# Two models in one kernel: convolution sums in PSUM, modulation products inside the input phase, tanh gates in the attention rounds, and other seams between the sublayers

## The chip, the cores and the metric

The kernel runs on one core of one Trainium2 chip, in one launch. The metric is the device time of that core in microseconds (us).

## The reference

Two models run one after the other on 256 tokens of 1024 numbers, all float32. The first has two layers. In each, one large product gives everything that its four branches need:

```python
h = x @ w_in[l]
(rw_p, rw_g, q_lat, kv_lat, k_pe, mla_g, conv_u, conv_g, xq, xg, merge) = jnp.split(h, SPLIT_POINTS, axis=-1)
y_rwkv = _rwkv7_branch(...)          # recurrent state over 256 steps
y_mla = _mla_branch(...)             # rms norm of two latents, then q, k, v, causal attention
y_conv = _conformer_conv_branch(...) # GLU, causal depthwise convolution of width 31, LayerNorm, swish
y_mem = _memory_xattn_branch(...)    # attention into 256 memory tokens
proj = jnp.einsum('bsnc,ncd->bsnd', branches, w_o_branch[l])
gates = jax.nn.sigmoid(merge.reshape(B, S, N_BRANCH, D) + b_gate[l])
merged = jnp.sum(gates * proj, axis=2)
x = _layer_norm(DEEPNORM_ALPHA * x + merged @ w_out[l], ln_g[l], ln_b[l])
```

The second model has two layers of three sublayers (a gated feed-forward, an attention mix, a gated feed-forward) over the tokens and a context of 256 rows. Each sublayer starts with an rms norm, is shifted and scaled by rows of a modulation product `silu(c) @ w_mod + b_mod` (nine rows for the tokens and nine for the context), and ends with `h + weight * gate * rms_norm(y)`.

## The kernel before

**First model.** All weights come in panels of 128 partitions by 2048 float32 (1 MB), 96 for each layer, in an order fixed ahead by `stream_of_a_layer`. The SP queue loads them into a ring of four slots (`m_ring`): a panel is fetched when the panel four places earlier has been used by PE (the semaphore `panel_used`). The products of two panels land in PSUM banks 0 and 1, taken in turn (`TURNS`, `USE`). PE waits on `bank_free0` or `bank_free1` until ACT or DVE has emptied the bank. Six other banks, A(0) to A(5), serve the attention, the norms and the recurrent branch.

A layer has these stages. The *input phase* takes 24 panels ("in"). ACT copies each to a rounded type (`high`, L755, to `m_ws`, three buffers), POOL subtracts that copy from the panel (L294), PE multiplies the two halves (`split_panel`, L377 to L379, 48 matmuls), and ACT moves the sum to `hT` (L780). Then comes a stretch in which the convolution's sum is finished by DVE (31 taps, L1007, four instructions for each tap in SBUF, begun during the input phase), and its norm and the norms of the latents run by turns on PE, ACT and DVE. After it come the products for q, k and v (`lat` panels), four attention rounds (two into the tokens, two into the memory), the preparation of the recurrent branch, its two halves, and a tail with the last gates.

The second model's modulation rows are worked out in the first model's layers: `mod_rows(w)` uses four "mod" panels with 32 columns of weights (PE L326, both banks, then ACT copies each bank to `mrow`), and `mod_columns(w)` turns two rows into columns (PE L337, ACT L735). Nine pairs of rows are taken in each layer: the first two in the stretch after the input phase, the others in the rounds and in the preparation. `gate(q, p)` (L346, a panel each) and `branch(q)` (L356, one panel) are the merge's products. DVE multiplies them (`merge`, L987) in the order of `MERGE_ORDER`.

**Second model.** 160 panels come through a ring of two. POOL rounds each (L1570) and subtracts (L1572). A sublayer starts with `norm_in`: DVE scales the tokens (L1997), PE makes rows (L1625) and transposes (L1633), ACT copies each of eight chunks, DVE rounds and subtracts each (L2001, L2003, semaphore `aT_split`). Then `hidden` runs the panels (L1616 to L1618, 48 matmuls for each). At the end, `norm_out` squares on ACT (L1864), takes the root (L1868) and lets DVE apply it (L2015) and add it to the tokens or to the context (L2019).

Of the kernel before, what the change touches and what calls it, by code (L numbers as in the profile page):

```python
# [32 lines left out]
MERGE_ORDER = (2, 3, 4, 5, 6, 7, 0, 1)  # L33


PANEL, USE, TURNS = {}, {}, [0, 0]
# [15 lines left out]
def stream_of_a_layer():  # L52

    def pair(w):
# [4 lines left out]
    feeds(*[("mem", n) for n in range(4)])  # L59
    feeds(*[("in", n) for n in range(24)])  # L60
    for n in list(range(4)):
        turn(n % 2, ("mem", n))
    for n in range(24):
        turn(n % 2, ("in", n))
    for w in range(PAIRS):
        if w == 2:
            feeds(*[("lat", n) for n in range(4)])
        pair(w)
        turn(w % 2, ("col", w))
    for q in MERGE_ORDER:  # L70
        feeds(("gate", q, 0), ("gate", q, 1), ("branch", q))
        for p in range(2):
            turn(p, ("gate", q, p))
        for b in range(2):
            turn(b, ("branch", q, b))
    feeds(*[("out", n) for n in range(4)])
# [82 lines left out]
def first_model(nc, io, x_tok, mod, out=None):  # L159

    with ExitStack() as ctx:  # L161
# [17 lines left out]
        small = sb("small", [P, 192])  # L179
        with ExitStack() as place:  # L180
            work = place.enter_context(nc.sbuf_tensor("m1_work", [P, 73 * T], F32))
# [22 lines left out]
        eps6, eps5, eps_gn = small[:, 180:181], small[:, 181:182], small[:, 182:183]  # L204
        ln_rows = hT[:, 20:28, :].rearrange("p u t -> p (u t)")
        mrow = brT[:, 0:KW, :].rearrange("p k t -> p (k t)")
# [5 lines left out]
        lat_sq, lat_n = units(44, 5), units(49, 5)  # L212
# [31 lines left out]
        def sgate(t):  # L244
# [4 lines left out]
            "slot0 slot1 slot2 slot3 loaded c_in c_act mcol_ps vec_in rows_in x_in out_st panel_used bank_free0 bank_free1 "  # L249
# [49 lines left out]
        def _(pe):  # L299
# [5 lines left out]
            with pe.Fori(0, DEPTH) as l:  # L305
# [106 lines left out]
                pe.wait_ge(s["c_act"], 1)  # L412
                mod_rows(0)
                pe.wait_ge(s["conv_acc"], l + 1)
                for k in range(KW):
                    last = mm(A(0)[:, 0:T], c("ones"), conv[:, k, :], start=(k == 0), stop=(k == KW - 1))
                last.then_inc(s["mean_ps"], 1)
                pe.wait_ge(s["csq_in"], l + 1)
                for k in range(KW):
                    last = mm(A(1)[:, 0:T], c("ones"), conv_sq[:, k, :], start=(k == 0), stop=(k == KW - 1))  # L420
                last.then_inc(s["var_ps"], 1)


                pe.wait_ge(s["lat_sq_in"], l + 1)
                pe.wait_ge(s["xT_sb"], 8 * l + 8)
                for j, (u0, n) in enumerate(((0, 3), (3, 2))):
                    for k in range(n):
                        last = mm(A(2)[:, j * T:(j + 1) * T], c("ones"), lat_sq[:, u0 + k, :],
                                  start=(k == 0), stop=(k == n - 1))
                last.then_inc(s["lat_ps"], 1)  # L430
                mod_columns(0)
                mod_rows(1)
                pe.wait_ge(s["lat_n_in"], l + 1)
# [5 lines left out]
                for h in range(HEADS):  # L439
                    out = A(1 + h // 2)[:, (h % 2) * T:(h % 2 + 1) * T]  # L440
# [6 lines left out]
                for h in range(HEADS):  # L447
# [6 lines left out]
                    if h % 4 == 3:  # L454
                        last.then_inc(s["k_ps"], 1)
                w = panel(("lat", 2))
# [12 lines left out]
                for a in range(4):  # L469
# [13 lines left out]
                    mod_columns((1, 3, 5, 6)[a])  # L483
                    mod_rows((2, 4, 6, 7)[a])
# [6 lines left out]
                    if a < 2:  # L491
                        mod_columns(2 + 2 * a)
                        mod_rows(3 + 2 * a)
# [13 lines left out]

                mod_columns(7)
                mod_rows(8)
# [9 lines left out]
                mod_columns(8)  # L519
                gate(2, 0)  # L520
                pe.wait_ge(s["o_done"], 4 * l + 4)
                pe.wait_ge(s["ksq_in"], l + 1)
# [4 lines left out]
                gate(2, 1)  # L527
                branch(2)
                gate(3, 0)
                gate(3, 1)  # L530
# [34 lines left out]
                for i in range(NT):  # L565
# [5 lines left out]
                    for g in range(4):  # L571
# [10 lines left out]
                        if g == 1:  # L582
                            gate(4 + i, i)
                        elif g == 3 and i == 0:
                            gate(4, 1)
                        elif g == 3:
                            branch(5)
# [43 lines left out]
                    if i == 0:  # L631
                        pe.wait_ge(s["conv_done"], l + 1)
                        branch(4)
                    else:
                        gate(6, 0)
# [26 lines left out]
                    gate(5 + i, i)  # L662
# [17 lines left out]
                branch(6)  # L680
                gate(7, 0)
# [6 lines left out]
                gate(7, 1)  # L688
                branch(7)
                gate(0, 0)  # L690
                gate(0, 1)
                pe.wait_ge(s["rw_done"], l + 1)
                branch(0)
                gate(1, 0)
                gate(1, 1)
# [15 lines left out]
        def _(act):  # L711
# [8 lines left out]
            with act.Fori(0, DEPTH) as l:  # L720
# [16 lines left out]
                def gate(q, p):  # L737
# [5 lines left out]
                    for u in range(2):  # L743
                        last = a_(sgate(t)[:, 2 * p + u, :], bank[:, p, u * T:(u + 1) * T], ACT.Sigmoid,
                                  bias=v("b_gate", q * 4 + p * 2 + u))
# [30 lines left out]
                for n in range(24):  # L776
                    if n + 2 < 24:
                        high(n + 2)
# [1449 lines left out]
```

## Time and profile before

| what | value |
|---|---|
| median of 3 runs | 3427.41 us (3423.55 to 3431.52) |
| the profiled execution | 3424.13 us, span 3421.9 us |
| PE busy | 2970.3 us, 87% |
| DVE, ACT, POOL busy | 1259.0, 706.6, 1256.1 us |
| mean granted clock of PE | 0.93 |
| layer 1: input phase | 42.3 to 179.0 us |
| layer 1: stretch between input phase and q | 179.0 to 240.1 us, PE busy 21.4 us |
| layer 1: q, k, v | 240.1 to 264.4 us |
| layer 1: four rounds | 264.4 to 347.5 us |
| layer 1: preparation | 347.5 to 426.6 us |
| layer 1: two halves | 426.6 to 585.9 us |
| layer 1: tail up to the output panels | 585.9 to 662.0 us |

The profile is of one execution, and its stages add up to its span. Layer 2 has the same stages at close to the same lengths (its stretch between input and q is 60.3 us). A stage is as long as the chain that runs through it, and PE's idle time in it says how far PE is from being that chain.

### The profile page before, as it was taken

To read this page: it belongs to the slowest core of one execution; us is meant where nothing else is said; L and a number is where in the kernel's file an instruction comes from. 1 tells how busy PE (TensorE), PEld (TensorE's weight loads), DVE (VectorE), ACT (ScalarE), POOL (GpSimd) and SP (SyncE) were. 2 spreads that over 40 slices of the span, in tenths; PEclk is the share of its full clock that TensorE was granted. 3 is DMA by queue.
4 is the path that set the end of the run, shared out by engine and by line. 5 is a ranking of instruction groups with operands and counts; after the bars stand their busy time and mean duration, and the time that the engine had idled before them with its cause. 6 is when DMAs were issued, how large, how long until landed. Compare 5 with 4: busy or idle time off the path is not lost.

```text
span 3421.9 us, 41743 instructions
## 1 busy us (share of the span) xinstructions
PE 2970.3 (87%) x16084; PEld 2443.6 (71%) x16084; DVE 1259.0 (37%) x1702; ACT 706.6 (21%) x1327; POOL 1256.1 (37%) x531
## 2 busy tenths in 40 slices
PE   8957799999577999599997988899979999697797
PEld 7934688789346886388775766688757878586695
DVE  2962734149628331400134163200341012515327
ACT  3413111033231110210112142211121111204211
POOL 4800000057000000266563503366544665371595
PEclk9978899999788999799998977999989999899899
DMA  6537411445383113322221202122221222130343
GB/s 220 186 140 291 152 62 62 147 168 186 133 304 149 51 62 123 112 98 97 82 92 53 94 1 68 49 98 98 86 74 67 94 97 86 62 111 25 111 172 123
DMA packets 67453, 383.80 MB, mean 112 GB/s; under 512 B 19072, under 2 KB 20736, under 8 KB 21888
## 3 DMA queue, kind: packets, MB, share of 16 engines
q1 hardware_dynamic: 66464, 379.19, 31.4%
q10 hardware_dynamic: 864, 2.84, 0.2%
q8 instruction: 91, 1.49, 0.2%
q14 instruction: 34, 0.28, 0.0%
HBM read 380.96 MB, written 1.05 MB: 112 GB/s over the span
## 4 chain that ended last, share of the span: by engine, by line
issue 32%; POOL 9%; POOLq 8%; PE 5%; DMA 2%; SPq 1%; DVE 1%; ACT 1%; DVEq 0%; ACTq 0%
POOL m_ws L1572 8%; POOLq L1571 7%; PE m_bank L1661 2%; DMA m_ring<-in_panels 2%; SPq L1525 1%; POOL m_ws L1590 1%; POOLq L1584 1%; POOLq L1589 1%; PE m_bank L1804 0%; PE m_bank L1616 0%; PE m_bank L1617 0%; PE m_bank L1618 0%; PE m_bank L1782 0%; PE m_bank L1769 0%; PE m_bank L1734 0%
## 5 line engine op out<-in xcount | busy, mean ns | idle before, releaser
L1616 PE MATMUL m_bank<-m_aT,m_ws 128*128 128x512 f32 (+1 forms) x1664 | 607.0, 365 | 52.3 <-DVE m_aT_low L2003 37.5
L1617 PE MATMUL m_bank<-m_aT_low,m_ws 128*128 128x512 f32 (+1 forms) x1664 | 603.8, 363 | 0.0
L1618 PE MATMUL m_bank<-m_aT,m_ws 128*128 128x512 f32 (+1 forms) x1664 | 603.2, 363 | 0.0
L1572 POOL TENSOR_TENSOR m_ws<-m_ring,m_ws 128x2048 fp32r<-128x2048 f32 x127 | 594.5, 4681 | 18.7
L1661 PE MATMUL m_bank<-m_ws,m_hs 128*128 128x512 f32 x1848 | 437.8, 399 | 38.5 <-DVE m_hs L2049 28.3
L294 POOL TENSOR_TENSOR m_ws<-m_ring,m_ws 128x2048 fp32r<-128x2048 f32 x48 | 225.0, 4692 | 624.3 <-ACT m_ws L755 624.2
L1661 PEld LDWEIGHTS m_bank<-m_ws,m_hs 128*128 128x128 f32 x1848 | 355.7, 193 | 120.4 <-issue 39.4
L1616 PEld LDWEIGHTS m_bank<-m_aT,m_ws 128*128 128x128 f32 x1664 | 317.3, 191 | 104.7 <-issue 34.2
L1583 POOL TENSOR_TENSOR m_small<-m_small 128x1 f32<-128x1 f32 x158 | 30.6, 194 | 923.1 <-PE m_bank L1618 503.2
L1618 PEld LDWEIGHTS m_bank<-m_aT,m_ws 128*128 128x128 f32 x1664 | 317.3, 191 | 48.1
L1617 PEld LDWEIGHTS m_bank<-m_aT_low,m_ws 128*128 128x128 f32 x1664 | 317.6, 191 | 47.6
L2040 DVE TENSOR_TENSOR m_hidT<-m_sg,m_bank 128x512 f32 (+1 forms) x88 | 54.6, 621 | 770.5 <-ACT m_sg L1879 770.5
L346 PE MATMUL m_bank<-m_xF,m_ring 128*128 128x256 f32 x1024 | 235.3, 391 | 43.0 <-DVE m_hT L987 40.4
L1570 POOL TENSOR_SCALAR m_ws<-m_ring 128x2048 fp32r<-128x2048 f32 x127 | 244.2, 1923 | 28.7 <-issue 19.9
L346 PEld LDWEIGHTS m_bank<-m_xF,m_ring 128*128 128x128 f32 x1024 | 198.9, 196 | 74.1 <-DVE m_hT L987 43.6
L1007 DVE SCALAR_TENSOR_TENSOR m_work<-m_work,m_vec 128x256 f32<-128x256 f32 x240 | 226.8, 1005 | 31.9 <-issue 31.9
L377 PE MATMUL m_bank<-m_xT,m_ws 128*128 128x256 f32 x768 | 216.0, 281 | 1.4 <-ACT m_work L773 1.4
L379 PE MATMUL m_bank<-m_xT,m_ws 128*128 128x256 f32 x768 | 217.1, 283 | 0.0
L2049 DVE TENSOR_TENSOR m_hs<-m_hidT,m_hs 128x512 fp32r<-128x512 f32 (+1 forms) x80 | 133.3, 1671 | 226.5 <-ACT m_hs L1888 226.4
L378 PE MATMUL m_bank<-m_xT_low,m_ws 128*128 128x256 f32 x768 | 213.5, 278 | 0.0
L1566 POOL MEMSET m_small<- 128x1 f32 x1 | 0.1, 98 | 538.9 <-POOLq L161 538.9
L377 PEld LDWEIGHTS m_bank<-m_xT,m_ws 128*128 128x128 f32 x768 | 144.3, 188 | 3.0 <-ACT m_work L773 3.0
(348 smaller groups left out, 3971.1 us busy)
## 6 DMA issues: line engine op xcount, KB each, us to landing
m_ring<-in_panels SPq DMA_DIRECT2D x352, 1024.0 KB, 4.8
m_bias<-in_rpb SPq DMA_DIRECT2D x48, 64.0 KB, 2.4
m_hT<-in_ln_rows ACTq DMA_DIRECT2D x2, 1024.0 KB, 6.4
m_con<-in_con SPq DMA_DIRECT2D x1, 1408.0 KB, 13.8
m_memT<-in_memT SPq DMA_DIRECT2D x1, 1024.0 KB, 5.9
x_tok<-in_x SPq DMA_DIRECT2D x1, 1024.0 KB, 14.4
m_ctx_tok<-in_ctx SPq DMA_DIRECT2D x1, 1024.0 KB, 4.8
out<-x_tok SPq DMA_DIRECT2D x1, 1024.0 KB, 4.0
```

Of the source, the lines that this page charges most:

```text
L294: nc.gpsimd.tensor_tensor(ws[:, c_ % 3, 1, :], ring[:, PANEL[("in", c_)] % RING, :], ws[:, c_ % 3, 0, :].bitcast(F32), ALU.subtract).then_ ...
L346: last = mm(out[:, u * T:(u + 1) * T], w[:, u, k, :], xF[:, k, :], start=(k == 0), stop=(k == KD - 1))
L377: mm(dst, w[:, 0, u, k, :], xT[:, k, :], start=(k == 0), stop=False)
L379: last = mm(dst, w[:, 1, u, k, :], xT[:, k, :], start=False, stop=(k == KD - 1))
L1007: V.scalar_tensor_tensor(conv[:, k, :], padded[:, k, bass.ds(tap, T)], vec[:, bass.ds(tap * KW + (VEC1["conv_w"] + k), 1)], conv[:, k, :], ...
L1570: nc.gpsimd.tensor_scalar(ws[:, p, 0, :], ring[:, p, :], 1.0, 0.0, ALU.mult, ALU.add)
L1571: pool.drain()
L1572: nc.gpsimd.tensor_tensor(ws[:, p, 1, :], ring[:, p, :], ws[:, p, 0, :].bitcast(F32), ALU.subtract)\
L1616: mm(out, w, a, start=start, stop=False)
L1617: mm(out, w, a_low, start=False, stop=False)
L1618: return mm(out, w_low, a, start=False, stop=stop)
L1661: last = mm(bank[:, 2 * i + hf, :], lhs[:, at], rhs[:, hf * 512:(hf + 1) * 512], start=start and q == 0, stop=stop and q == 2)
```

## The change

1. The order of the panels and of the banks' turns is new. Rows 0 to 3 of the modulation are taken inside the input phase, after input panels 3, 7, 11 and 15, and columns 0 to 3 after panels 5, 9, 13 and 18. Rows 4 come between the products for k and v, rows 5 to 8 in rounds 2 and 3 and in the preparation. Gates and branches 4 and 5 are taken in rounds 0 and 1, and `MERGE_ORDER` follows.
2. The sums of the latents' squares are taken on PE after input panel 8, the convolution's mean after 19 and its variance after 21. Their roots on ACT and the rest on DVE follow inside the input phase. Some buffers move to a new tile `ext`, so that nothing is shared that is still in use.
3. The convolution's running sum lies in A(0) and A(1), in PSUM. The last tap writes to SBUF.
4. A gate is the tanh of half its argument, and the merge multiplies (gate + 1) by the product. The residual's factor is doubled and the epsilon of the layer norm is four times as large, so that the result is the same.
5. Second model: the first panel of each sublayer runs k outside and u inside (`first_unit_panel`), and waits for the first two of the eight chunks rather than for all. `norm_out` keeps the product in its PSUM bank and adds it from there, and starts with a square root of a constant.
6. The scratch area for generated descriptors is set to 1024.

```diff
+MERGE_ORDER = (4, 5, 2, 3, 6, 7, 0, 1)
+ROWS_AFTER, COLUMNS_AFTER = (3, 7, 11, 15), (5, 9, 13, 18)
...
+    for n in range(24):
+        feeds(("in", n))
+        turn(n % 2, ("in", n))
+        if n in ROWS_AFTER:
+            rows(ROWS_AFTER.index(n))
+        if n in COLUMNS_AFTER:
+            columns_of(COLUMNS_AFTER.index(n))
...
                 for n in range(24):
                     split_panel(n, free(("in", n))).then_inc(s["panel_used"], 1)
-
+                    if n in ROWS_AFTER:
+                        pe.wait_ge(s["c_act"], 1)
+                        mod_rows(ROWS_AFTER.index(n))
+                    if n in COLUMNS_AFTER:
+                        mod_columns(COLUMNS_AFTER.index(n))
...
+                mod_rows(7)
+                gate(2, 0)
                 mod_columns(7)
-                mod_rows(8)
+                gate(2, 1)
 
                 pe.wait_ge(s["tanh_in"], l + 1)
...
                 pe.wait_ge(s["o_done"], 4 * l + 4)
+                branch(2)
                 pe.wait_ge(s["ksq_in"], l + 1)
...
                 for n in range(24):
-                    if n + 2 < 24:
+                    if n + 2 < 24 and n + 1 not in ROWS_AFTER:
                         high(n + 2)
+                    if n - 1 in ROWS_AFTER:
+                        mod_rows(ROWS_AFTER.index(n - 1))
+                    if n - 1 in COLUMNS_AFTER:
+                        mod_columns(COLUMNS_AFTER.index(n - 1))
                     used(("in", n))
                     a_(hT[:, 2 * n:2 * n + 2, :], bank[:, n % 2, :].rearrange("p (u t) -> p u t", t=T),
                        ACT.Copy if n < 16 else ACT.Silu).then_inc(bank_free[n % 2], 1)
+                    if n + 1 in ROWS_AFTER:
+                        high(n + 2)
...
                         V.scalar_tensor_tensor(tap_sum(k), padded[:, k, bass.ds(tap, T)],
                                                vec[:, bass.ds(tap * KW + (VEC1["conv_w"] + k), 1)], tap_sum(k),
                                                ALU.mult, ALU.add)
...
+            def first_unit_panel(e, b, tokens):
+
+                w = ws[:, b, :, :].rearrange("p h (u k c) -> p h u k c", u=2, k=KD)
+                for k in range(KD):
+                    pe.wait_ge(s["aT_split"], KD * e + max(k, 1) + 1)
+                    for u in range(2):
+                        last = parts(bank[:, u, 0:tokens[u]], w[:, 0, u, k, :], w[:, 1, u, k, :],
+                                     aT[:, k, 0:tokens[u]], aT_low[:, k, 0:tokens[u]], k == 0, k == KD - 1)
+                return last
...
             def norm_out(e, tiles, last_panel):
+                a_(small[:, 62:63], eps, ACT.Sqrt)
...
-                        V.tensor_tensor(tok(i), tok(i), y[:, i, :], ALU.add).then_inc(s["x_new"], 1)
+                        V.tensor_tensor(halves(tok(i)), halves(tok(i)), bank[:, 2 * i:2 * i + 2, :], ALU.add)\
+                            .then_inc(s["x_new"], 1)
```

The first place is ACT's queue around input panel 3, of the kernel before. `m_ws<-m_ring` is the rounding of a coming input panel, `m_hT<-m_bank` the emptying of a bank, and "slot" waits are for a load.

```order
L755 ACTIVATE m_ws<-m_ring 128x2048 [waits m1_slot0]
L722 REGISTER_ALU
L780 ACTIVATE m_hT<-m_bank 128x512 [waits m1_panel_used]
L755 ACTIVATE m_ws<-m_ring 128x2048 [waits m1_slot1]
L722 REGISTER_ALU
L780 ACTIVATE m_hT<-m_bank 128x512 [waits m1_panel_used]
L784 ACT_TABLE_LOAD
L784 ACTIVATE m_hT<-m_hT 128x1024
L755 ACTIVATE m_ws<-m_ring 128x2048 [waits m1_slot2]
L722 REGISTER_ALU
L780 ACTIVATE m_hT<-m_bank 128x512 [waits m1_panel_used]
```

In the changed kernel two roundings (of input panels 4 and 5) stand ahead of the emptying of panel 3's bank, and a third (of panel 6) ahead of the copies of the modulation rows (`m_ext<-m_bank`).

```order
L800 ACTIVATE m_ws<-m_ring 128x2048 [waits m1_slot0]
L800 ACTIVATE m_ws<-m_ring 128x2048 [waits m1_slot1]
L766 REGISTER_ALU
L829 ACTIVATE m_hT<-m_bank 128x512 [waits m1_panel_used]
L835 ACT_TABLE_LOAD
L835 ACTIVATE m_hT<-m_hT 128x1024
L800 ACTIVATE m_ws<-m_ring 128x2048 [waits m1_slot2]
L766 REGISTER_ALU
L773 ACTIVATE m_ext<-m_bank 128x512 [waits m1_panel_used]
L766 REGISTER_ALU
L773 ACTIVATE m_ext<-m_bank 128x512 [waits m1_panel_used]
```

The second place is PE's queue behind the 48 matmuls of input panel 3, in the changed kernel. Before, the wait on `split_in` and the matmuls of panel 4 stood there directly.

```order
L349 REGISTER_ALU [waits m1_c_act]
L355 REGISTER_ALU [waits m1_slot0]
L366 MATMUL m_bank<-m_ring,m_cact 32x512 [waits m1_bank_free0]
L366 MATMUL m_bank<-m_ring,m_cact 32x512 x3
L366 MATMUL m_bank<-m_ring,m_cact 32x512 [waits m1_slot1]
L366 MATMUL m_bank<-m_ring,m_cact 32x512 x3
L355 REGISTER_ALU [waits m1_slot2]
L366 MATMUL m_bank<-m_ring,m_cact 32x512 [waits m1_bank_free1]
L366 MATMUL m_bank<-m_ring,m_cact 32x512 x3
L366 MATMUL m_bank<-m_ring,m_cact 32x512 [waits m1_slot3]
L366 MATMUL m_bank<-m_ring,m_cact 32x512 x3
L355 REGISTER_ALU
```

Now sixteen products of the modulation and their waits stand ahead of panel 4: two for loads whose slots come free late, and one for each bank.

The third place is the start of a sublayer's first panel on PE. Before, one wait for all chunks stands ahead of it:

```order
L1648 UNCONDITIONAL_BRANCH [waits m2_aT_split]
L1648 ISA
L1616 MATMUL m_bank<-m_aT,m_ws 128x512 [waits m2_h_free,m2_split_in]
L1617 MATMUL m_bank<-m_aT_low,m_ws 128x512
L1618 MATMUL m_bank<-m_aT,m_ws 128x512
```

In the changed kernel it waits for each chunk, and the first wait is for two:

```order
L1681 MATMUL m_bank<-m_aT,m_ws 128x512 [waits m2_aT_split,m2_h_free,m2_split_in]
L1682 MATMUL m_bank<-m_aT_low,m_ws 128x512
L1683 MATMUL m_bank<-m_aT,m_ws 128x512
L1681 MATMUL m_bank<-m_aT,m_ws 128x512
L1682 MATMUL m_bank<-m_aT_low,m_ws 128x512
L1683 MATMUL m_bank<-m_aT,m_ws 128x512
L1681 MATMUL m_bank<-m_aT,m_ws 128x512 [waits m2_aT_split]
L1682 MATMUL m_bank<-m_aT_low,m_ws 128x512
L1683 MATMUL m_bank<-m_aT,m_ws 128x512
L1681 MATMUL m_bank<-m_aT,m_ws 128x512
```

The waits moved from the head of the panel to the six matmuls of each chunk.

## Rows read from the trace of the kernel before

**Rows 1.** PE timeline, 179 to 240 us: start, duration, operation, idle before, releaser.

```profile
180.73 2.78 PE L326 MATMUL m_bank<-m_ring,m_cact 128*32 128x512 f32 x24
...
211.72 3.78 PE L416 MATMUL m_bank<-m_work,m_con 128*128 128x256 f32 x8 [26.63 <-DVEq L1011]
...
224.55 1.84 PE L337 MATMUL m_bank<-m_con,m_brT 128*128 128x2 f32 x16
...
240.11 12.32 PE L442 MATMUL m_bank<-m_work,m_ring 128*128 128x256 f32 x48 [9.71 <-DVE m_work L1033]
```

**Rows 2.** Ring loads issued at 179.2, 183.7 and 185.3 us: time to landing.

```profile
DMA to landing us min/median/max: 4.8/4.8/4.8
...
DMA to landing us min/median/max: 8.1/8.1/8.1
...
DMA to landing us min/median/max: 9.0/9.0/9.0
```

**Rows 3.** ACT timeline in the input phase, 145 to 152 us.

```profile
145.46 1.91 ACT L755 ACTIVATE m_ws<-m_ring 128x2048 fp32r<-128x2048 f32 x1
150.65 0.60 ACT L780 ACTIVATE m_hT<-m_bank 128x512 f32<-128x512 f32 x1 [3.28 <-PE m_bank L379]
```

**Rows 4.** DVE timeline, convolution taps with POOL busy, then idle.

```profile
159.74 9.77 DVE L1007 SCALAR_TENSOR_TENSOR m_work<-m_work,m_vec 128x256 f32<-128x256 f32 x4 [0.54 <-issue]
...
172.25 1.67 DVE L1007 SCALAR_TENSOR_TENSOR m_work<-m_work,m_vec 128x256 f32<-128x256 f32 x4 [0.53 <-issue]
```

**Rows 5.** Page, part 5: the convolution taps of both layers.

```profile
L1007 DVE SCALAR_TENSOR_TENSOR m_work<-m_work,m_vec 128x256 f32<-128x256 f32 x240 | 226.8, 1005 | 31.9 <-issue 31.9
```

**Rows 6.** PE timeline, RWKV preparation of layer 1.

```profile
354.90 2.96 PE L516 MATMUL m_bank<-m_work,m_lora 64*128 64x256 f32 x16
...
370.72 1.89 PE L524 MATMUL m_bank<-m_work,m_con 128*128 128x256 f32 x8
...
404.27 15.63 PE L346 MATMUL m_bank<-m_xF,m_ring 128*128 128x256 f32 x64 [17.84 <-DVE m_hT L987]
...
426.64 1.91 PE L303 MATMUL m_bank<-m_con,m_work 128*128 128x128 f32 x16
```

**Rows 7.** DVE timeline: the key norm's wait in the preparation.

```profile
374.19 0.69 DVE L1109 TENSOR_SCALAR m_work<-m_work 128x1024 f32<-128x1024 f32 x1 [6.41 <-ACT m_work L860]
```

**Rows 8.** PE timeline, the end of layer 1's gates.

```profile
616.49 14.08 PE L346 MATMUL m_bank<-m_xF,m_ring 128*128 128x256 f32 x64 [0.78 <-DVE m_hT L987]
630.40 7.07 PE L356 MATMUL m_bank<-m_brT,m_ring 128*128 128x256 f32 x32
```

**Rows 9.** PE timeline, one sublayer seam of the second model.

```profile
1820.16 5.57 PE L1625 MATMUL m_bank<-m_prob,m_con 128*128 128x512 f32 x8 [17.25 <-DVE m_prob L1987]
...
1837.74 0.80 PE L1616 MATMUL m_bank<-m_aT,m_ws 128*128 128x512 f32 x1 [7.88 <-DVE m_aT_low L2003]
```

**Rows 10.** DVE timeline of that seam.

```profile
1804.12 7.63 DVE L2019 TENSOR_TENSOR x_tok<-x_tok,m_y 128x1024 f32<-128x1024 f32 x2
...
1815.48 2.36 DVE L2019 TENSOR_TENSOR m_ctx_tok<-m_ctx_tok,m_y 128x1024 f32<-128x1024 f32 x2
...
1830.38 0.69 DVE L2003 TENSOR_TENSOR m_aT_low<-m_hidT,m_aT 128x512 fp32r<-128x512 f32 x1
```

**Rows 11.** POOL timeline of that seam.

```profile
1805.39 5.28 POOL L1572 TENSOR_TENSOR m_ws<-m_ring,m_ws 128x2048 fp32r<-128x2048 f32 x1
1850.53 0.19 POOL L1583 TENSOR_TENSOR m_small<-m_small 128x1 f32<-128x1 f32 x1 [39.86 <-PE m_bank L1618]
```

**Rows 12.** Windows of that seam: span, PE busy, granted clock, DMA share.

```profile
1824.00:1834.00 10.00, 5.45 (x36) 1.00 0.01 2
1834.00:1842.00 8.00, 4.26 (x12) 0.57 0.00 0
```

**Rows 13.** ACT timeline: the table load ahead of the norm's square root.

```profile
1798.68 1.28 ACT L1868 ACT_TABLE_LOAD   x1
```

**Rows 14.** Page, part 5: PE idle before the first panels of the sublayers.

```profile
L1616 PE MATMUL m_bank<-m_aT,m_ws 128*128 128x512 f32 (+1 forms) x1664 | 607.0, 365 | 52.3 <-DVE m_aT_low L2003 37.5
```

More of the change, by code:

```diff
@@ L52, in stream_of_a_layer, with rows @@
 def stream_of_a_layer():
-    def pair(w):
+    def rows(w):
         feeds(*[("mod", 4 * w + n) for n in range(4)])
@@ L57, in pair, with columns_of, gates @@
             turn(b, ("row", 2 * w + b))
[L59 to L68, printed above, removed]
+    def columns_of(w):
         turn(w % 2, ("col", w))
-    for q in MERGE_ORDER:
+    def gates(q):
         feeds(("gate", q, 0), ("gate", q, 1), ("branch", q))
@@ L75, in stream_of_a_layer @@
             turn(b, ("branch", q, b))
+    feeds(*[("mem", n) for n in range(4)])
+    for n in range(4):
+        turn(n % 2, ("mem", n))
+    for n in range(24):
[5 more added lines that the diff above has]
+            columns_of(COLUMNS_AFTER.index(n))
+    feeds(("lat", 0), ("lat", 1))
+    rows(4)
+    feeds(("lat", 2), ("lat", 3))
+    columns_of(4)
+    gates(4)
+    gates(5)
+    for w in (5, 6):
+        rows(w)
+        columns_of(w)
+    rows(7)
+    turn(0, ("gate", 2, 0))
+    columns_of(7)
+    turn(1, ("gate", 2, 1))
+    for b in range(2):
+        turn(b, ("branch", 2, b))
+    feeds(("gate", 2, 0), ("gate", 2, 1), ("branch", 2))
+    rows(8)
+    turn(0, ("gate", 3, 0))
+    columns_of(8)
+    turn(1, ("gate", 3, 1))
+    for b in range(2):
+        turn(b, ("branch", 3, b))
+    feeds(("gate", 3, 0), ("gate", 3, 1), ("branch", 3))
+    gates(6)
+    for q in (7, 0):
+        for p in range(2):
+            feeds(("gate", q, p))
+            turn(p, ("gate", q, p))
+    feeds(("branch", 7), ("gate", 1, 0), ("gate", 1, 1), ("branch", 0), ("branch", 1))
+    for name in (("branch", 7), ("gate", 1), ("branch", 0), ("branch", 1)):
+        for b in range(2):
+            turn(b, name + (b,))
     feeds(*[("out", n) for n in range(4)])
@@ L421, in _ @@
[L421 to L432, printed above, removed]
@@ L1104, in _ @@
                 V.memset(AR[64:128, :, :, 2, :], 0.0)
+                merge(2)
+                dve.wait_ge(s["wa_in"], l + 1)
+                for k in range(KW):
+                    V.tensor_scalar(k2[:, k, :], sa[:, k, :], 1.0, v("k_a", k), ALU.subtract, ALU.mult)
                 dve.drain()
@@ L1723, in _ @@
                         pe.wait_ge(s["f_free"], 8 * l + n - 1)
-                    unit_panel((n0 + n) % 2, 2 * (n % 2), [T2 if full or 2 * n + u >= F_AK else T for u in range(2)])\
-                        .then_inc(s["used"], 1)
+                    tokens = [T2 if full or 2 * n + u >= F_AK else T for u in range(2)]
+                    if n == 0:
+                        last = first_unit_panel(e, n0 % 2, tokens)
+                    else:
+                        last = unit_panel((n0 + n) % 2, 2 * (n % 2), tokens)
+                    last.then_inc(s["used"], 1)
                 for n in range(2):
```

259 lines of the change are left out of this document (144 added, 115 removed).

## The prediction

> **What bounds the kernel now.** I read the page first, then PE's timeline by stages, then the waits where PE stands. PE is busy 87% of the span, so most of the time is PE's own work, and only the stretches where it stands can give anything. Layer 1 has four kinds. The stretch of 61.1 us behind the input phase (60.3 in layer 2) holds 21.4 us of PE work: PE waits 26.63 us for the end of the convolution on DVE, then for the norm [rows 1]. The rounds and the preparation of the recurrent branch are chains on DVE and ACT, with one hole of 17.84 us [rows 6]. In the tail PE runs gates and branches back to back [rows 8]. In the second model each seam between sublayers leaves PE standing 17.25 us for the norm of the last product and 7.88 us for the eight chunks [rows 9].
>
> **First model, input phase.** This is where the change can lose. The order shows four modulation panels between input panels 3 and 4, and the ring holds four panels. I count from the moment PE ends input panel 3, t = 0. The 16 products cost 2.78 / 24 x 32 = 3.7 us of PE [rows 1]. A lone load lands after 4.8 us; issued behind others it takes 8.1 and 9.0 us, and as these two were issued 1.6 us apart, each lands 2.5 us behind the one before it [rows 2]. At t = 0.15 the slot of panel 3 is refilled with the fourth "mod" panel, landing at 5.0. The first two are used by 1.0 and 1.9, so input panel 4 is issued at 1.15 and lands at 7.5, and panel 5, issued at 2.05, at 10.0. ACT's queue has the rounding of 4 (7.55 to 9.45) and of 5 (10.05 to 11.95), 1.91 us each, ahead of the emptying of panel 3's bank, 0.60 us [rows 3]. So bank 1 is free at 12.6, and the third and fourth "mod" products run from 12.6 to 14.5. Only then are the slots for input panels 6 and 7 free: panel 6 is issued at 13.75 and lands at 18.6. Its rounding, to 20.5, stands ahead of the copy of the modulation row, which frees bank 0 at 21.1. PE starts input panel 4 at 21.2. POOL's part of panel 4, with the 5.28 us of such an instruction [rows 11], is over by 15 and does not decide. With the columns, 1.84 us and their wait, 2.2 in all [rows 1], an insertion costs 23.4 us, of which some 6 are work. Four make 93.6.
>
> The latents' sums, mean and variance cost 2.2, 1.9 and 1.9 us of PE in the phase (10 matmuls of the L416 kind, and 4 each: the row has eight in 3.78 us, at the lower clock [rows 1]). After such a gap I expect the clock to come back late: the gates behind the 17.84 us hole took 15.63 us against 14.08 for the same 64 matmuls [rows 6, 8], so 1.6 for each gap, 6.4. The phase grows by 93.6 + 6.0 + 6.4 + 0.7 of small hand-overs = 106.7 us, the stretch of 61.1 goes, and 1.9 of transposes stay: **q starts 47.5 us later**.
>
> The convolution's place in PSUM earns nothing here. Even at the mean of 1005 ns [rows 5], the 120 instructions of a layer take 113 us of DVE beside the input phase that now lasts 243, and the mean is asked for only after panel 19. That cover is thick: without it, the taps under POOL at 9.77 us for four against 1.67 [rows 4] would stand in the way as before.
> The Trainium skill (SBUF — State Buffer, the section on its two separate sides) says that a VectorE instruction with two SBUF inputs and a GpSimd one lock each other out for the whole instruction; the tap in PSUM has one SBUF input and so escapes, which the two rows for four taps fit.
>
> **First model, the rest.** Between k and v the four products of rows 4 cost 3.7, and the two last "lat" panels are issued only as they free slots: they land 8.5 and 11.0 after the products' start by the spacing above, which costs waits of 4.8 and 0.9: +9.4. In the rounds gates and branches take the place of modulation products under the waits for the softmax; two gates, 14.1, are a little longer than the cover, and I take +1.4 between -5 and +5. In the preparation, L516 stood 7.4 us behind the rounds' end (354.90 - 347.5). Now rows 7 (3.7), gate(2,0) (7.07), a column pair (1.84) and gate(2,1) (7.07) stand ahead, 19.7 us, and about 3.9 for the landing of gate(2,0)'s panel: 23.6. Behind it come L516 (2.96), branch(2) (7.07), L524 (1.89) and ACT's 1.1 to the start of DVE's chain at 374.19: 36.6. From there to 426.64 it was 52.45 [rows 6, 7], less merge(2), 1.3, now ahead: 87.8, with 0.2 of hand-over 88.0 against 79.1: +8.9. The clock after the hole: +1.6. In the second half branch(5), 7.07 [rows 8], goes from a place where DVE's masks cover a part: between 0 and 7.07, I take half, -3.6. The tail loses four gate panels and one branch, five times 7.07: -35.3. Sum for a layer: 47.5 + 9.4 + 1.4 + 8.9 + 1.6 - 3.6 - 35.3 = +29.9, **two layers +60** (bounds +35 and +80: stalls of 18 and 24 us for 21.2, the preparation from 0 to +12). The tanh gates change no count that PE or ACT waits for.
>
> **Second model.** At a seam the first panel started at 1837.74 and ended at 1850.5, 12.8 us, because the clock was at 0.57 from 1834 to 1842 [rows 9, 11, 12], after PE had stood 7.88 us. Now it starts when the second chunk is split, at 1830.38 + 0.69 = 1831.1 [rows 10], while the clock is 1.00 (1824 to 1834), and DVE delivers a chunk each 1.1 us against 1.35 that PE takes for one (10.8 for the panel at full clock), so PE never waits again. It ends at 1842.3: 8.2 earlier. Five sublayers show this wait, 37.5 us together [rows 14]; four are like this one (32.8), the first gives about 6, the sixth waits for another thing: -38.8. In `norm_out` the addition to the tokens took 7.63 us under POOL's 5.28 and that to the context 2.36 without it [rows 10, 11]. With the product in PSUM it should take the short time, but the small two-input operations of the next pair of tiles then stand where POOL's instruction still runs, until 1810.7: I take 1.8 of the 5.3, four times, -7.2. The dummy root pulls the table load, 1.28 [rows 13], off the last norm: -1.3, and -0.2 for small things. **Second model -47.5** (bounds -35 and -54).
> By the rule of the Trainium skill named above, the addition is free of the lock and the next small one is not; the sum would be the same -7.2.
>
> Sum: 3424.1 + 59.8 - 47.5 = 3436.4 for an execution like the profiled one. The runs' median lies 3.3 above it, so **3440 us**.
>
> **The rivals.**
> (A) As worked out, 3433 to 3450. For it: ACT's order is fixed, and each step is a row. 0.5.
> (B) The refill is shorter. If two loads issued 0.9 us apart don't queue, panel 5 lands at 6.9 and each insertion costs 18.1 + 2.2, 8 x 3.1 = 25 less: 3415. If the clock also stays up, 8 x 1.6 = 13 less: 3402. Against it: the 8.1 and 9.0 us [rows 2]. This one ends faster. It decides from a stall of 20.4 us for each insertion downward if no other term moves by more than 10. 0.15.
> (C) The seam gives all of the 5.3 us four times, 14 more: 3426, the same as before. For it: the context's 2.36; against it: POOL's instruction still runs. 0.13.
> (D) The change does not stall: if the rounding of panels 4 and 5 came early, an insertion would cost its work, about 9 us, and 8 x 14.4 = 115 less gives 3325. It would need a ring that holds more than the order shows. 0.05.
> (E) More is lost: landings of 9.0 us in the rounds too (gate and branch panels are taken at 7.07 each, three in a row), 8 more for each layer, or table loads of 1.28 by turns between silu, root and tanh inside the phase, about four for each layer: 3455 to 3465. 0.17.
>
> **How the numbers follow.** This kernel's measurement tells 0.2%, 6.9 us. Faster (below 3420.5): B and D, and some of C: 0.22. Same: C and the low edge of A: 0.18. Slower: the rest of A, and E: 0.60. The range from 3404 to 3464 takes in A, C, most of B and of E.
>
> **What the new profile should show.** Between input panels 3 and 4 PE has two gaps, the first of about 10 us before the third "mod" product, the second of about 7 us, ended by ACT's copy of a row. Input phases of about 243 us. No idle stretch for the convolution. The tail 35 us shorter. The first panels of sublayers start about 6.6 us earlier, at full clock. I am wrong if the gap is not near 21 us, if DVE's convolution ends after panel 19, or if the seams give less than 6 us each.

## The result and the profile after

The changed kernel takes 3473.45 us (median of 4 runs, 3467.78 to 3474.25), against 3426.64 us before (4 runs): a ratio of 1.0132, with an interval of 1.0114 to 1.0149. It is 46.8 us slower, outside the range that I gave. The head of the page after:

```profile
span 3465.8 us, 41711 instructions
...
PE 2986.7 (86%) x16084; PEld 2461.0 (71%) x16084; DVE 1118.9 (32%) x1705; ACT 710.5 (20%) x1335; POOL 1248.8 (36%) x531
```

PE has 44 us more span and 16 us more busy time. By stages of layer 1, read from PE's timelines of both kernels (the last column is from the prediction):

| stage, layer 1 | before | after | difference | predicted |
|---|---|---|---|---|
| first input panel to q | 197.9 | 256.1 | +58.2 | +47.5 |
| q, k, v | 24.3 | 35.9 | +11.7 | +9.4 |
| four rounds | 83.1 | 83.3 | +0.2 | +1.4 |
| preparation | 79.2 | 91.4 | +12.2 | +10.5 |
| halves and tail | 235.4 | 199.4 | -36.0 | -38.9 |
| output panels, and the start | | | -3.1 | 0 |
| sum | | | +43.2 | +29.9 |

Up to the second model's first row products the whole first model is 89.3 us longer (1487.74 against 1398.45 us), so layer 2 loses 46.1. From there to the end it is 1978.1 against 2023.4 us: -45.4, predicted -47.5.

**The insertion.** PE's timeline of the changed kernel between input panels 3 and 4 (start, duration, operation, idle before and its releaser):

```profile
63.67 1.92 PE L366 MATMUL m_bank<-m_ring,m_cact 128*32 128x512 f32 x16
77.24 3.59 PE L366 MATMUL m_bank<-m_ring,m_cact 128*32 128x512 f32 x16 [11.65 <-ACT m_hT L829]
86.71 0.58 PE L417 MATMUL m_bank<-m_xT,m_ws 128*128 128x256 f32 x1 [5.88 <-ACT m_ext L773]
```

Two "mod" products, a hole of 11.65 us, two more, a hole of 5.88 us, and then panel 4: 23.0 us after panel 3's end at 63.74. The order of events was predicted with 10.7 and 6.7 us. ACT's timeline of the same place tells who held PE:

```profile
72.32 1.91 ACT L800 ACTIVATE m_ws<-m_ring 128x2048 fp32r<-128x2048 f32 x1 [13.59 <-DMA m_ring<-in_panels]
74.79 1.91 ACT L800 ACTIVATE m_ws<-m_ring 128x2048 fp32r<-128x2048 f32 x1 [0.57 <-DMA m_ring<-in_panels]
76.61 0.58 ACT L829 ACTIVATE m_hT<-m_bank 128x512 f32<-128x512 f32 x1
...
84.19 1.91 ACT L800 ACTIVATE m_ws<-m_ring 128x2048 fp32r<-128x2048 f32 x1 [4.58 <-DMA m_ring<-in_panels]
86.00 1.07 ACT L773 ACTIVATE m_ext<-m_bank 128x512 f32<-128x512 f32 x2
```

L800 rounds panels 4 and 5. It waited 13.59 us for the load of the first, and 0.57 for that of the second. Only then comes L829, which empties bank 1, though PE's sum had been lying there since 63.74. L800 of panel 6 stands ahead of the two copies of the modulation rows (L773) in the same way. Panel 4 landed 8.6 us after panel 3's end (I had 7.5), panel 5 11.05 (I had 10.0). The waits of the whole kernel, by who ends them (sum, times, longest):

```profile
PE m_bank L1690 <- DVE m_prob L2075: 98.9, 6, 26.1
PE m_bank L366 <- ACT m_hT L829: 88.1, 8, 11.8
PE m_bank L417 <- ACT m_ext L773: 47.8, 8, 6.4
```

There are 88.1 + 47.8 = 135.9 us in sixteen holes of a kind that was not there before. The windows show the clock (span, PE busy, granted clock, DMA share, GB/s; 1.00 is 2.4 GHz, 0.50 is 1.2 GHz, and a value between them is the mean of a window that holds both):

```profile
40.00:64.00 24.00, 23.31 (x197) 1.00 0.48 175
64.00:77.00 13.00, 1.60 (x16) 0.75 0.61 242
...
86.71:90.90 4.19, 4.19 (x19) 0.50 0.04 16
90.90:94.00 3.10, 3.10 (x29) 1.00 0.00 0
...
155.70:159.20 3.50, 3.50 (x19) 0.51 0.45 187
```

For the first 4.2 us of input panel 4 PE is busy without a pause at a granted clock of 0.50, and then it is 1.00. So input panels 4 and 5 took 13.45 us where two panels take 11.4. The last row is another place: there PE has waited only 0.69 us, but the sixteen narrow products of a column pair (L377, 2 columns each, 1.94 us) stand just before it.

**Behind the input phase.** PE's timeline around k and v:

```profile
296.95 10.60 PE L485 MATMUL m_bank<-m_ext,m_ring 128*128 128x256 f32 x48 [0.56 <-DVE m_work L1097]
...
320.64 1.93 PE L366 MATMUL m_bank<-m_ring,m_cact 128*32 128x512 f32 x8 [3.33 <-DMA m_ring<-in_panels]
326.12 1.19 PE L506 MATMUL m_bank<-m_ring,m_ext 128*128 128x512 f32 x1 [3.54 <-DMA m_ring<-in_panels]
```

Rows 4 take four ring slots, so the last of them and the "lat" panels are waited for, 3.33 and 3.54 us. In the preparation the first gate waits for its load, and L569 (L516 before) starts 25.6 us after the rounds' end at 416.16, where 23.6 was predicted and 7.4 stood before [rows 6]:

```profile
423.85 7.17 PE L386 MATMUL m_bank<-m_xF,m_ring 128*128 128x256 f32 x32 [1.51 <-DMA m_ring<-in_panels]
...
441.78 2.96 PE L569 MATMUL m_bank<-m_work,m_lora 64*128 64x256 f32 x16 [1.54 <-ACT m_work L908]
444.67 7.17 PE L396 MATMUL m_bank<-m_brT,m_ring 128*128 128x256 f32 x32
...
507.56 0.69 PE L343 MATMUL m_bank<-m_con,m_work 128*128 128x128 f32 x2 [22.33 <-DVEq L1232]
```

**The convolution.** DVE's timelines, first a tap (89.00 to 90.66 us), then the POOL instruction that runs beside it (86.18 to 90.73), then the last tap and the mean:

```profile
89.00 1.66 DVE L1066 SCALAR_TENSOR_TENSOR m_bank<-m_work,m_vec,m_bank 128x256 f32<-128x256 f32 x4 [0.57 <-issue]
```

```profile
86.18 4.55 POOL L334 TENSOR_TENSOR m_ws<-m_ring,m_ws 128x2048 fp32r<-128x2048 f32 x1 [2.87 <-ACT m_ws L800]
```

```profile
150.50 1.66 DVE L1071 SCALAR_TENSOR_TENSOR m_work<-m_work,m_vec,m_bank 128x256 f32<-128x256 f32 x4 [0.66 <-issue]
...
270.34 1.42 DVE L1089 SCALAR_TENSOR_TENSOR m_work<-m_bank,m_work 128x256 f32<-128x256 f32 x4 [105.74 <-PE m_bank L465]
```

A tap of four instructions takes 1.66 us with the sum in PSUM, beside POOL's instruction and without it, against 9.77 and 1.67 in SBUF [rows 4]. The sum is ready at 152 us. Then DVE waits 105.74 us (the latents' norm in between), until PE comes to the mean behind panel 19.
This agrees with the Trainium skill (SBUF — State Buffer, the section on the two separate sides, under "Who interferes with whom"): outside the two-port modes, a VectorE instruction with at most one SBUF input does not contend with GpSimd.

**The second model.** The same seam as in [rows 9, 10, 12], on PE, on DVE, on POOL, on ACT, and by windows:

```profile
1899.00 5.86 PE L1690 MATMUL m_bank<-m_prob,m_con 128*128 128x512 f32 x8 [15.04 <-DVE m_prob L2075]
...
1910.34 0.47 PE L1681 MATMUL m_bank<-m_aT,m_ws 128*128 128x512 f32 x1 [1.36 <-DVE m_aT_low L2091]
```

```profile
1883.91 2.35 DVE L2107 TENSOR_TENSOR x_tok<-x_tok,m_bank 128x1024 f32<-128x1024 f32 x2
...
1886.48 4.49 DVE L179 TENSOR_TENSOR m_small<-m_small 128x2 f32<-128x2 f32 x1
...
1894.32 2.35 DVE L2107 TENSOR_TENSOR m_ctx_tok<-m_ctx_tok,m_bank 128x1024 f32<-128x1024 f32 x2
```

```profile
1886.45 4.51 POOL L1637 TENSOR_TENSOR m_ws<-m_ring,m_ws 128x2048 fp32r<-128x2048 f32 x1
```

```profile
1867.67 1.28 ACT L1946 ACT_TABLE_LOAD   x1
```

```profile
1900.00:1910.00 10.00, 8.57 (x40) 0.83 0.00 0
1910.00:1914.00 4.00, 3.66 (x16) 1.00 0.01 4
1914.00:1922.00 8.00, 8.00 (x37) 1.00 0.00 0
```

The wait ahead of the first panel is 1.36 us rather than 7.88, the clock of that panel is 1.00 rather than 0.57, and the addition to the tokens takes 2.35 us rather than 7.63. The wait for the norm is 15.04 rather than 17.25, 2.2 us less. Two things make it. ACT's table load now stands 16 us ahead of the end of PE's last product (4.2 us before [rows 13]), so DVE starts the norm's chain 1.3 us earlier against the end of that product. The chain itself, from DVE's first instruction to PE's start, is 18.9 us rather than 19.9 (1800.30 to 1820.16 before, 1880.07 to 1899.00 after): of the 5.3 us that the addition gives back, a small two-input instruction of the next pair of tiles (2 elements in each partition, others of its kind take 0.16 us) loses 4.3. It ends 0.01 us after POOL's.

### The profile page after: what moved, and what is told of

It is laid out like the page before. It is cut to its first block, busy times and chain, and to the rows that moved or that the text cites. A ratio compares the mean times of both kernels' runs of the same rounds, so it can differ in the third digit from the quotient of the medians.

```text
span 3465.8 us, 41711 instructions
## 1 busy us (share of the span) xinstructions
PE 2986.7 (86%) x16084; PEld 2461.0 (71%) x16084; DVE 1118.9 (32%) x1705; ACT 710.5 (20%) x1335; POOL 1248.8 (36%) x531
## 4 chain that ended last, share of the span: by engine, by line
issue 30%; POOL 9%; POOLq 8%; PE 5%; DMA 2%; SPq 1%; DVE 1%; ACT 1%; DVEq 0%; ACTq 0%
POOL m_ws L1637 8%; POOLq L1636 7%; PE m_bank L1744 2%; DMA m_ring<-in_panels 2%; POOLq L1649 1%; SPq L1590 1%; POOL m_ws L1655 1%; POOLq L1654 1%; PE m_bank L1891 0%; PE m_bank L1681 0%; PE m_bank L1683 0%; PE m_bank L1682 0%; PE m_bank L1869 0%; PE m_bank L1856 0%; PE m_bank L1822 0%
## 5 line engine op out<-in xcount | busy, mean ns | idle before, releaser
L1637 POOL TENSOR_TENSOR m_ws<-m_ring,m_ws 128x2048 fp32r<-128x2048 f32 x127 | 592.5, 4665 | 18.7
L334 POOL TENSOR_TENSOR m_ws<-m_ring,m_ws 128x2048 fp32r<-128x2048 f32 x48 | 218.3, 4556 | 788.7 <-ACT m_ws L800 788.7
L417 PE MATMUL m_bank<-m_xT,m_ws 128*128 128x256 f32 x768 | 229.4, 299 | 52.9 <-ACT m_ext L773 47.8
L386 PE MATMUL m_bank<-m_xF,m_ring 128*128 128x256 f32 x1024 | 230.3, 384 | 10.4 <-DMA m_ring<-in_panels 7.4
L418 PE MATMUL m_bank<-m_xT_low,m_ws 128*128 128x256 f32 x768 | 224.8, 293 | 0.0
L419 PE MATMUL m_bank<-m_xT,m_ws 128*128 128x256 f32 x768 | 224.5, 292 | 0.0
L417 PEld LDWEIGHTS m_bank<-m_xT,m_ws 128*128 128x128 f32 x768 | 156.1, 203 | 68.6 <-issue 65.4
L366 PE MATMUL m_bank<-m_ring,m_cact 128*32 128x512 f32 x576 | 84.4, 717 | 98.0 <-ACT m_hT L829 88.1
```

What stands on the lines that cost most here:

```text
L334: nc.gpsimd.tensor_tensor(ws[:, c_ % 3, 1, :], ring[:, PANEL[("in", c_)] % RING, :], ws[:, c_ % 3, 0, :].bitcast(F32), ALU.subtract).then_ ...
L386: last = mm(out[:, u * T:(u + 1) * T], w[:, u, k, :], xF[:, k, :], start=(k == 0), stop=(k == KD - 1))
L417: mm(dst, w[:, 0, u, k, :], xT[:, k, :], start=(k == 0), stop=False)
L418: mm(dst, w[:, 0, u, k, :], xT_low[:, k, :], start=False, stop=False)
L419: last = mm(dst, w[:, 1, u, k, :], xT[:, k, :], start=False, stop=(k == KD - 1))
L1637: nc.gpsimd.tensor_tensor(ws[:, p, 1, :], ring[:, p, :], ws[:, p, 0, :].bitcast(F32), ALU.subtract)\
```

## The experiments

The column "before" is the kernel before, run beside each. Times are medians. The ratios, with their 95% intervals, are taken over all executions, and can differ a little from the quotient of the medians.

| kernel | us | before | ratio |
|---|---|---|---|
| changed first model alone | 3526.06 | 3429.14 | 1.029 (1.0261 to 1.0318) |
| changed second model alone | 3375.38 | 3429.14 | 0.9849 (0.9831 to 0.9867) |
| changed kernel, ACT reordered | 3402.07 | 3429.14 | 0.9921 (0.9904 to 0.9937) |
| convolution in PSUM alone | 3367.39 | 3429.14 | 0.9814 (0.9797 to 0.9831) |
| convolution in PSUM and second model | 3315.56 | 3427.26 | 0.9672 (0.9656 to 0.9688) |
| these, and the norms inside | 3310.26 | 3427.26 | 0.9646 (0.9623 to 0.9669) |
| changed kernel, rows behind the input phase | 3331.53 | 3427.26 | 0.9718 (0.9702 to 0.9735) |
| first panels alone | 3385.26 | 3427.26 | 0.9872 (0.9856 to 0.9889) |
| last norm alone | 3407.38 | 3427.10 | 0.995 (0.9936 to 0.9963) |
| single insertions | 3308.91 | 3426.18 | 0.9649 (0.9628 to 0.9669) |

**The two models apart.** All edits of the diff in the second model undone, or made alone.

> The changed first model with the second model of the kernel before. If the two models' changes add up, the first is worth +89 us by the two profiles (PE's first row product of the second model starts at 1487.74 us against 1398.45), so about 3515 us. The rival, that the changed seams of the second model carry part of the loss (their gain was counted at 45 us and could be less because something else became slower), gives less than 3500.

> The first model of the kernel before with the changed second model. The two profiles give the second model 2023.4 us before and 1978.1 after, so -45 us: about 3381 us. The rival gives more than 3395.

Measured +96.9 and -53.8 us. They add up to +43.1, against 46.8 for both, so nothing is lost between them: the first model is the whole loss. Both are larger than the profiles' +89 and -45, but that need not be an effect of the edits. In the profile of the second model alone, that model takes 1979.6 us, 43.8 less than before, and the unchanged first model 1393.8 rather than 1398.5. In the profile of the first model alone, the first model takes 1496.6 rather than the changed kernel's 1487.7, with the same code, and the unchanged second 2029.6 rather than 2023.4. So the same code moves by 5 to 9 us between executions.

**ACT's order.** The panels, the ring and PE's order stay as in the changed kernel.

```diff
 for n in range(24):
-    if n + 2 < 24 and n + 1 not in ROWS_AFTER:
+    if n + 2 < 24 and n + 1 not in ROWS_AFTER and n not in ROWS_AFTER:
         high(n + 2)
-    if n - 1 in ROWS_AFTER:
-        mod_rows(ROWS_AFTER.index(n - 1))
...
-    if n + 1 in ROWS_AFTER:
-        high(n + 2)
+    if n in ROWS_AFTER:
+        mod_rows(ROWS_AFTER.index(n))
+        high(n + 1)
+        high(n + 2)
```

> The changed kernel, with ACT's queue alone reordered: after input panels 3, 7, 11 and 15 it first empties the bank of that panel, then copies the two modulation rows, and only then rounds the next two input panels. Theory 1, that the stall of 22 to 23 us at each insertion is made by ACT's order (rounding waits for loads, emptying waits behind it): the third and fourth modulation products follow at once, input panel 4 waits only for its own load (8.6 us after panel 3), its rounding (1.9) and POOL (4.6), so it starts at about 15 instead of 23. Eight insertions give -60, and PE's shorter pause may give up to -10 more: 3405 to 3415 us. Rival, that the ring's four slots make the stall whatever ACT does (the loads of input panels 4 and 5 land late and POOL's two subtractions follow): less than -20, 3455 us or more.

Measured 3402.07 us, 71 less than the changed kernel's 3473.45. PE's timeline:

```profile
64.48 2.78 PE L366 MATMUL m_bank<-m_ring,m_cact 128*32 128x512 f32 x24
69.57 1.07 PE L366 MATMUL m_bank<-m_ring,m_cact 128*32 128x512 f32 x8 [2.31 <-DMA m_ring<-in_panels]
78.95 0.58 PE L417 MATMUL m_bank<-m_xT,m_ws 128*128 128x256 f32 x1 [8.31 <-POOL m_ws L334]
```

The first hole is 2.31 us, for a load, and the second 8.31 us, for POOL's subtraction. Panel 4 starts 14.4 us after panel 3's end at 64.55, where 15 was expected. Over the eight places the stalls shrink from 180 to 117 us, so ACT's order made some 8 us of each, and 63 of the 71 us gained. The remaining 14 to 16 are load, rounding and subtraction in a row, that is, the ring.

**The convolution's sum in PSUM, alone.**

```diff
-with dve.Fori(1, CONV_K) as tap:
+with dve.Fori(1, CONV_K - 1) as tap:
     for k in range(KW):
-        V.scalar_tensor_tensor(conv[:, k, :], ..., conv[:, k, :], ALU.mult, ALU.add)
+        V.scalar_tensor_tensor(tap_sum(k), ..., tap_sum(k), ALU.mult, ALU.add)
```

> The kernel before with one part of the change alone: the convolution's running sum in PSUM. In the changed kernel the four instructions of a tap take 1.66 us also while POOL works, against up to 9.77 before, so the sum ends inside the input phase, and the wait of 26.6 us of PE for it goes in both layers: -50 us, about 3377 us. My prediction took it as earning nothing, which was so only because the mean is asked for late in the changed order. Rival: the next things of the stretch (the four loads of modulation panels, the norm's chain) take the place of the wait: less than -20, 3407 us or more.

Measured -61.8 us, where 50 were expected. The wait for the convolution [rows 1] is gone, and q starts at 207.99 rather than 240.11. Most of the rest is the clock: the products behind the missing wait run at full clock, the eight of L416 in 2.00 us rather than 3.78:

```profile
183.84 2.00 PE L416 MATMUL m_bank<-m_work,m_con 128*128 128x256 f32 x8
...
207.99 1.62 PE L442 MATMUL m_bank<-m_work,m_ring 128*128 128x256 f32 x3 [9.71 <-DVE m_work L1040]
```

**With the second model.** Both parts that gain alone, nothing else.

> The kernel before with the convolution's sum in PSUM and the changed second model, and nothing else of the change. The two alone gave -62 and -54 us. If they are independent (different stretches of the program), they add up: about 3313 us. A value above 3330 would speak for something shared.

Measured 3315.56 us, -111.7: they add up.

**The norms inside the input phase as well,** with the modulation's rows left behind it.

> As the kernel with both of these parts, and also the sums of the latents, the mean and the variance inside the input phase as in the change; the modulation's first two row pairs stay behind the input phase. With the sum in PSUM the stretch between input and q is 30.1 us in layer 1. The products move in for about 6 us of PE, and what is left is 1.9 of transposes, 3.9 + 1.8 + 3.6 of modulation and some 2 of waits, so about 13 + 6 = 19 against 30: -11 for each layer, about 3291 us. Rival: the root and the squares on ACT with their table loads, or the longer input phase's clock, eat it: 3305 us or more.

Measured 3310.26 us. The intervals of the two ratios overlap, so a gain over the former is not shown, and the expected -22 is wrong in any case. The stretch behind the input phase is shorter, but q now waits for its own panels:

```profile
189.53 1.06 PE L329 MATMUL m_bank<-m_ring,m_cact 128*32 128x512 f32 x8 [0.46 <-DMA m_ring<-in_panels]
...
206.08 12.28 PE L446 MATMUL m_bank<-m_ext,m_ring 128*128 128x256 f32 x48 [4.03 <-DMA m_ring<-in_panels]
```

The eight "mod" panels ahead of the "lat" ones are used no faster than they are loaded, and the slots for "lat" come free behind them. The wait for the norm has become a wait for the ring (4.03 us), which I had not counted, though it comes from the same four slots as the insertion's.

**The rows behind the input phase.** The changed kernel with all four pairs of rows and columns behind the 24 input panels.

```diff
-ROWS_AFTER, COLUMNS_AFTER = (3, 7, 11, 15), (5, 9, 13, 18)
+ROWS_AFTER, COLUMNS_AFTER = (), ()
...
                 transpose_x(2)
+                for w in range(4):
+                    mod_rows(w)
+                    mod_columns(w)
```

> The changed kernel with one thing undone: the four pairs of modulation rows and their columns are not inserted between input panels but stand all together behind the input phase (the same 32 loads and products). Theory 1, an insertion costs the latency of refilling the split panels (load 4.8 or more, rounding 1.9, POOL 4.6) again each time, and a low clock behind it: behind the input phase the same loads stream at about 2.5 us each, 35 to 45 us in all, so the way from the first input panel to q takes 136.8 + 6 + 1.9 + 40 = 185 us against 256, -71 for each layer: about 3331 us. Rival: the loads as such are the price (40 panels of 1 MB in the phase), wherever they stand: then 3450 us or more.

Measured 3331.53 us, to 0.5 us what was expected, and 142 less than the changed kernel. PE's timeline behind the input phase, where the loads stream and each "mod" product waits for them about a microsecond at most:

```profile
187.78 1.06 PE L369 MATMUL m_bank<-m_ring,m_cact 128*32 128x512 f32 x8 [0.45 <-DMA m_ring<-in_panels]
...
209.50 1.07 PE L369 MATMUL m_bank<-m_ring,m_cact 128*32 128x512 f32 x8 [1.06 <-DMA m_ring<-in_panels]
...
224.81 1.62 PE L492 MATMUL m_bank<-m_ext,m_ring 128*128 128x256 f32 x3 [1.53 <-DMA m_ring<-in_panels]
```

The transposes end at 184.62 and q starts at 224.81: 40.2 us for sixteen panels that made the input phase 112 us longer (253.8 us in the changed kernel, 141.6 here; both hold the norms' products). The same loads, products and copies are done; only their place differs. This kernel is still 21 us slower than the one with the norms inside (3310.26 us). It has four pairs of rows ahead of q rather than two, another order of gates and branches, and the tanh. Which of these makes the 21 us was not taken apart, so the tanh gates stay untested.

**The second model's two edits apart.**

> The kernel before with the sublayers' first panel started at the second chunk, without the change of the second model's last norm. My term for it is -38.8 us: about 3390 us. Rival, that the panel starts earlier but waits for chunks or runs at the low clock: -20 us or less.

> The kernel before with the second model's last norm alone changed (the product stays in PSUM and is added from there, a square root of a constant ahead). My term is -7.2 for four additions and -1.5 for the rest: about -9 us, 3420 us. If the whole 5.3 us of each addition came back, it would be -22, about 3407 us; if small two-input instructions behind it wait for POOL all the same, less than -5.

Measured -42.0 for the first panels (expected -38.8) and -19.7 for the last norm, where 9 were expected (by the ratio -17, with -12.7 to -21.9). The waits of the kernel with the last norm alone:

```profile
PE m_bank L1625 <- DVE m_prob L1988: 99.3, 6, 26.3
```

They are 7.5 us shorter than before's 106.8 together: the first, ahead of which nothing was changed, is 26.3 rather than 24.3, and the five others, behind a changed norm, are 73.0 rather than 82.5. So the norms give 9.5 us at the seams. In its profile the second model takes 2010.3 us, 13.1 less, and the unchanged first model 1394.0, 4.5 less than before. The edit is therefore worth 9.5 to 13 us as far as the traces show; the 3.6 between these are not accounted for, and what stands above them is of the size by which unchanged code moves. The sum of the two edits, -61.7, against -53.8 for both together, is within the intervals of the three.

**Single insertions.** The kernel with the norms inside, and the eight panels of the first two pairs of rows taken one at a time, behind input panels 1, 4, 7, 10, 13, 16, 19 and 22, with their sums in A(3) and A(4).

> As the kernel with norms inside the input phase (3310 us), but the eight modulation panels of the first two pairs are inserted one at a time, behind input panels 1, 4, 7, ..., 22, and their sums lie in A(3) and A(4), so that no bank of the input products is held. Theory 1 says that an insertion stalls PE by the refill of the ring only where more than one foreign panel stands in a window of four: an input panel is loaded, rounded and split 11.4 us after its slot comes free, and with one foreign panel between them PE has 2 x 5.7 + 0.9 = 12.3 us of other work, so there is no stall. The input phase grows by 8 x 0.93 + 2 = 9.5 us to about 152, and behind it only the transposes stand before q: q starts at about 196 instead of 206, -8 to -10 for each layer, about 3292 us. Rival: each insertion stalls as the four at once did, by at least 5 us: then 8 x 5 = +40 for each layer, 3370 us or more.

Measured 3308.91 us. The mechanism holds; the gain doesn't. Most insertions now cost their product and nothing more, as the first one:

```profile
52.42 1.06 PE L359 MATMUL m_bank<-m_ring,m_cact 128*32 128x512 f32 x8
53.42 0.39 PE L400 MATMUL m_bank<-m_xT,m_ws 128*128 128x256 f32 x1
```

Only the pair of columns in bank 0 still makes PE wait long, for ACT, which has the rounding of a later panel, and a wait of 3.28 us for its load, ahead of the copy:

```profile
129.20 1.95 PE L349 MATMUL m_bank<-m_con,m_brT 128*128 128x2 f32 x16
135.44 0.58 PE L400 MATMUL m_bank<-m_xT,m_ws 128*128 128x256 f32 x1 [4.29 <-ACT mod L762]
```

q starts at 206.65, as late as in the kernel with the norms inside (206.08). The single insertions save 17 us behind the input phase, and they add 19 inside it: eight products, the columns with 6 us, two waits for POOL of 1.5 us together, and a panel at the lower clock behind the columns (0.50 from 132 to 138 us).

## Why the prediction was wrong

**The sign, the place and the mechanism were right.** I had a slower kernel, by a stall at each insertion made by the ring and by ACT's order, and a second model that gives back part of it. Both were tested one by one.

**The size was too small: 3439.7 predicted, 3473.4 measured, 33.7 us apart.** The terms, for both layers, each from the stage table and the timelines:

- *The clock behind an insertion* ("1.6 for each gap, 6.4"). In layer 1 PE worked 25.4 us of the input panels at 0.50, where a matmul starts every 0.213 us rather than every 0.119, which costs 11.3 us: 4.9 a layer more than I had, 9.8 in all. Behind the four insertions it is 18.6 us at 0.50 and a cost of 8.3, so 2.1 for each gap rather than 1.6. The other 3.0 arise in two places where I had no term: behind the column pairs at 153.5 and 258.3 us, where PE had waited less than a microsecond (the row of 155.70 above). I took the price from one gap of 17.84 us. This term had no bounds of its own.
- *The stall* ("21.2"): 23.0, 22.9, 21.8 and 21.8 in layer 1, 4.7 a layer more, 9.4 in all. In the first of them the loads land 1.1 us later than by the spacing that I took, and the third and fourth "mod" products, at 0.50, take 3.6 us rather than 1.9; the second hole is 0.8 shorter. This lay inside the stall's bounds of 18 to 24.
- *Small hand-overs* ("0.7"): the phase grew by 117.0 us; four stalls took 89.5, columns 9.3, norms 4.6 and the clock 11.3. The rest is 2.3: 3.2 in all.
- *Halves and tail* (-38.9, measured -36.0): 5.8. *q, k, v* (+9.4, measured +11.7): 4.6. *Preparation* (+10.5, measured +12.2): 3.4.
- Layer 2 as I bound it lost 2.9 us more than layer 1 (1.8 of them are PE's wait for the second model's first norm, 26.1 against 24.3), the second model gained 2.1 less than predicted, and the median lies 5.7 above the profiled run and not 3.3: 7.4 together.
- Against it: rounds, output panels, columns and norms' products, -10.4 in all.

These make 33.2 of the 33.7 us. The failed step is the sum of the first model, "two layers +60 (bounds +35 and +80)", which measured +89. In it the clock's term (6.4 a layer, measured 11.3) and the stall (21.2, measured 22.4 in the mean) are each between 9 and 10 us too small. The bounds were also drawn too tight for the terms that they name: a stall of 24 alone gives +82, and with a preparation of +12 it is +89.

**The rivals.** (B) and (D) are refuted by the timeline; (C) by the wait of 15.04 us, where (C) needs 12. (E) said that more would be lost, but at other places. The rounds, where it had the landing of loads, moved by 0.2 us. The table loads inside the phase cost PE nothing that can be seen: in the kernel with the rows behind, which has the same norms inside, the phase is 141.6 us against 136.8, and the norms' products make up the difference.

**The convolution** "earns nothing here" fits the changed kernel's timeline, though no run has that kernel with the sum in SBUF, and it hid the larger finding. Alone it gives 62 us, because there PE takes the mean at once. The change takes the mean behind panel 19 of a phase that the insertions have stretched, so the sum lies ready for over 100 us. So its gain can't show there: the wait that it removes no longer exists.

**The second model's term** was right in size, -45.4 in the profile and -53.8 by the runs alone, for -47.5, but for the norm partly by luck. That a small two-input instruction behind the addition would wait for POOL's came true (4.49 us at 1886.48). It leaves 0.9 us at a seam where I had 1.8. The table load, which I took off the last norm only (-1.3), comes off the chain of each norm, so the seam's 2.2 us came out near my 1.8 for another reason.

## What to carry to other kernels

A ring of four loads is also a pipeline: each panel that another engine must prepare needs its slot early enough, and as many foreign panels as the ring has slots empty the pipeline. It then starts again with load, rounding and subtraction in a row. One foreign panel in a window of four cost little more than its own product here; the same panels in one block behind the phase cost the rate of the loads.
In an in-order queue, put what frees a bank for another engine ahead of what waits for a load.
A change of several parts is worth measuring part by part: two parts of this one gain 112 us together, and the rest takes some 160 back.

## What was unexpected of the hardware

The granted clock was 0.50 over 3.4 us in which PE was busy all the time (155.8 to 159.2 us), with only one hole, of 0.69 us, in the 19 us before them, but just behind sixteen products of two columns each. And it was 1.00 from 82 to 84 us, when PE stood idle in the second hole of the insertion, and back at 0.50 when panel 4 started at 86.71.
DVE's multiply and add with the running sum in PSUM took 1.66 us for four, beside POOL's subtraction and without it, and no longer than the same in SBUF with POOL idle (1.67).
A DVE instruction on 2 elements in each partition took 4.49 us beside a POOL instruction that had started 0.03 us before it (1886.48 us), and 0.16 us elsewhere.
